# The last weight's first head in two passes of 128 tokens, in a one-core kernel of two transformer blocks

## What is computed

```python
def peer(x, w_q, sub_keys, expert_u, expert_v):
    q = (x @ w_q).reshape(B, S, 8, 2, 128)                      # 8 heads, two sides
    s = jnp.einsum('bshpk,hpnk->bshpn', q, sub_keys)            # 128 scores a side
    top_s, top_i = lax.top_k(s, 16)
    cand_s = top_s[..., 0, :, None] + top_s[..., 1, None, :]    # 256 pairs
    best_s, pos = lax.top_k(cand_s.reshape(B, S, 8, 256), 16)
    ids = (top_i[..., 0, :, None] * 128 + top_i[..., 1, None, :]) at pos
    g = jax.nn.softmax(best_s)
    # for each token, over its 8 * 16 = 128 experts:
    act = jax.nn.gelu(jnp.einsum('td,tkd->tk', x, expert_u[ids])) * g
    return jnp.einsum('tk,tkd->td', act, expert_v[ids])
```

## Time and profile before

| | |
|---|---|
| median of three runs | 3479.82 us (3477.35 to 3481.0) |
| the profiled execution, its own time | 3478.45 us |
| its span in the profile | 3476.6 us |
| TensorE clock granted, mean | 0.992 of 2.4 GHz |
| last split weight's matmuls end | about 2115.5 us |
| peer_w_q on TensorE | 2115.5 to about 2252.5 us |
| first gather issued | 2144.89 us |

### The profile page before, as it was taken

How to read it: one execution, slowest core, us unless ns; L and a number is a source line. 1 busy time by engine, 2 the same in 40 slices (tenths; PEclk the granted TensorE clock), 3 DMA queues, 4 the chain that set the end, 5 groups by cost and what they waited for, 6 DMA issues and landing times.

```text
span 3476.6 us, 34930 instructions
## 1 busy us (share of the span) xinstructions
PE 3131.9 (90%) x13518; PEld 2280.5 (66%) x13518; DVE 2235.2 (64%) x3468; ACT 1251.9 (36%) x1845; POOL 540.9 (16%) x533
## 2 busy tenths in 40 slices
PE   7999999999999999999999999898777767777776
PEld 6998998888877888888888888743222223222222
DVE  7786777775556777775557675757767554444444
ACT  5554566554435455554346752111111110000001
POOL 0000000000000000000000001535343333333332
PEclk9999999999999999999999999999999999999999
DMA  6554555556554655556565557999999999999998
GB/s 214 160 157 154 158 176 170 175 163 205 188 181 151 194 188 180 190 191 206 189 201 189 169 194 267 393 404 406 420 420 420 420 420 421 420 420 420 420 420 344
DMA packets 405740, 936.92 MB, mean 269 GB/s; under 512 B 16487, under 2 KB 246536, under 8 KB 339144
## 3 DMA queue, kind: packets, MB, share of 16 engines
q0 software_dynamic: 75936, 547.39, 38.3%
q1 hardware_dynamic: 328624, 386.96, 34.7%
q10 hardware_dynamic: 1016, 0.35, 0.0%
HBM read 932.54 MB, written 2.10 MB: 269 GB/s over the span
## 4 chain that ended last, share of the span: by engine, by line
PE 62%; DMA 28%; DVE 6%; POOL 2%; issue 1%; ACT 1%; POOLq 0%; ACTq 0%; SPq 0%; DVEq 0%
DMA Ub<-in_peer_u,ids 28%; PE W L1269 14%; PE W L1277 11%; PE W L1279 11%; PE W L1278 11%; PE W L1267 7%; DVE Ub L2324 4%; PE M L1330 1%; PE M L1419 1%; PE T L1419 1%; POOL Ub L2408 1%; PE W L1266 1%; DMA Vb<-in_peer_v,ids 1%; POOL Vb L2418 1%; PE W L1238 0%
## 5 line engine op out<-in xcount | busy, mean ns | idle before, releaser
L1901 DVE TENSOR_TENSOR wl<-raw,wh 128x1024 fp32r<-128x1024 f32 (+1 forms) x720 | 843.8, 1187 | 560.2 <-ACT wh L1502 558.3
L1502 ACT ACTIVATE wh<-raw 128x1024 fp32r<-128x1024 f32 (+1 forms) x720 | 730.2, 1029 | 754.3 <-PE W L1279 568.5
L2324 DVE CUSTOM_DVE_ANT_0 Ub<-Ub,xn 128x2048 f32<-128x2048 f32 x256 | 586.2, 2291 | 481.8 <-DMA Ub<-in_peer_u,ids 481.6
L1269 PE MATMUL W<-u,wh 128*128 128x512 f32 x2040 | 725.0, 398 | 0.0
L1419 PE MATMUL W<-Vb,diag 128*128 128x512 f32 x1008 | 465.3, 605 | 164.3 <-DMA Vb<-in_peer_v,ids 108.6
L1267 PE MATMUL W<-u,wl 128*128 128x256 f32 x2176 | 604.6, 283 | 4.6 <-DVE u L1863 4.6
L1277 PE MATMUL W<-wh,u 128*128 128x512 f32 (+1 forms) x1280 | 485.9, 380 | 1.2 <-DVE u L2252 1.0
L1279 PE MATMUL W<-wh,u 128*128 128x512 f32 (+1 forms) x1280 | 477.7, 373 | 0.0
L1278 PE MATMUL W<-wl,u 128*128 128x512 f32 (+1 forms) x1280 | 477.3, 373 | 0.0
L1419 PEld LDWEIGHTS W<-Vb,diag 128*128 128x128 f32 x1008 | 182.8, 191 | 446.7 <-issue 365.3
L1269 PEld LDWEIGHTS W<-u,wh 128*128 128x128 f32 x2040 | 384.8, 189 | 88.9
(11 more groups left out here) (332 smaller groups left out, 3022.2 us busy)
## 6 DMA issues: line engine op xcount, KB each, us to landing
raw<-in_w_in SPq DMA_DIRECT2D x128, 1024.0 KB, 5.3
raw<-in_w_up SPq DMA_DIRECT2D x88, 1024.0 KB, 5.4
raw<-in_w_down SPq DMA_DIRECT2D x44, 1024.0 KB, 5.0
raw<-in_w_in SPq DMA_DIRECT2D x144, 256.0 KB, 3.6
raw<-in_w_out SPq DMA_DIRECT2D x32, 1024.0 KB, 5.1
raw<-in_w_proj_a SPq DMA_DIRECT2D x16, 1024.0 KB, 5.0
Wb<-in_peer_w_q SPq DMA_DIRECT2D x16, 1024.0 KB, 9.4
raw<-in_w_proj_b SPq DMA_DIRECT2D x4, 1024.0 KB, 5.1
```

The costliest lines, as they stand in the source:

```text
L1269: i = q.matmul(o, vh, u[:, :, kk, :], start=False, stop=last)
L1502: q.activation(wh[:, s % NS, 0:b.half], r, ACT.Copy).then_inc(s_hi, 1)
L1901: q.tensor_tensor(wl[:, s % NS, 0:b.half], r, wh[:, s % NS, 0:b.half].bitcast(F32), SUB).then_inc(s_lo, 1)
L2324: q.tensor_tensor_reduce(U[:, :], U[:, :], xn[:, t, :], 1.0, 0.0, MUL, ADD, dots[t][:, k:k + 1]).then_inc(s_dot, 1)
```

## The change

Head 0 is taken out of the loop over the heads. `first_head` runs its 32 weight tiles twice, once with the first 128 tokens moving and once with the other 128. After the first pass ScalarE copies (`first_out`), TensorE makes the scores (`first_scores`, two matmuls), ScalarE keeps them (`first_keep`), and the first choice starts. `xn` is made in two halves, four pieces ahead and four (`second_xn`) when both passes are laid. `top_ids` treats both sides in one instruction each. Two more slots for chunks of peer_w_q lie over xn's second half and the second half of the scores; so chunks 0 and 1 go there, chunks 2 to 4 to the raw slots, 5 to 8 to the other four, and chunk i from 9 on waits for chunk i-7 as before.

```diff
-NW = 7
+NW = 9
+NWR = 7
@@ Plan
-        for i in range(8):
+        for j in range(4):
             yield "DVE", lambda: t
-            self.done("xn", self.put("DVE", 0.7, t, "xn", i % 2, i // 2))
-            if i < 7:
-                del self.ready["xn"]
+            self.done(("xn", 0, j), self.put("DVE", 0.7, t, "xn", 0, j))
+
+    def second_xn(self):
+        for j in range(4):
+            t = yield "DVE", lambda: self.when("first head")
+            self.done(("xn", 1, j), self.put("DVE", 0.7, t, "xn", 1, j))
@@ out_wq
-        if h == 0:
-            self.start((1, 0), self.choose(0, 0))
...
+    def first_head(self):
+        n = self.next_block
+        b = self.blocks[n]
+        self.until(lambda: self.pair_free[n % 2])
+        for t in range(2):
+            if t:
+                self.until(lambda: self.free(0.0, self.T0, self.T1))
+                self.first = self.T0.take(1), self.T1.take(1)
+            for k0 in range(0, 16, 2):
+                self.until(lambda: self.when(("turned", "u5", k0 // 2)))
+                self.pump()
+                s = b.first + k0 // 4
+                ready = max(self.loaded(s), self.when(("turned", "u5", k0 // 2)), self.pair_free[n % 2] if t == 0 else 0.0)
+                self.taken[s] = self.put("PE", 4 * 0.224, ready, "first", t, k0)
+            if t == 0:
+                self.pair_free[n % 2] = None
+            self.start((0, n), self.out_first(n, t, self.clock["PE"]))
+        self.done("first head", self.clock["PE"])
+        self.next_block += 1
+
+    def out_first(self, n, t, end):
+        yield "ACT", lambda: end
+        x = self.put("ACT", 0.5, end, "first_out", t)
...
+        x = yield "PE", lambda: None if self.when("keys") is None else self.free(x, bank)
...
+        x = self.done(("score", 0), self.put("PE", 0.45, x, "first_scores", t))
+        yield "ACT", lambda: None if self.when("peer") is None else x
+        bank.free = self.done(("sc0", t), self.put("ACT", 0.45, x, "first_keep", t))
+        if t == 0:
+            del self.ready["score", 0]
+            self.start((1, 0), self.choose(0, 0))
@@ choose
-        self.done(("ids", t, h), self.put("DVE", 3.6, r, "top_ids", t, h))
+        self.done(("ids", t, h), self.put("DVE", 3.1, r, "top_ids", t, h))
@@ lay
         self.start((2, 0), self.begin(128 - NU))
-        for h in range(8):
+        self.first_head()
+        self.start((1, 5), self.second_xn())
+        for h in range(1, 8):
             self.stream(("wq", h))
@@ sync
-                    if i < NR:
-                        e.wait_ge(s_lo, 2 * (c - NR) + 2)
+                    if i == 0:
+                        e.wait_ge(s_kym, 4)
+                    elif i == 1:
+                        e.wait_ge(*pair_done(("res", 2, 0)))
+                    elif i < 2 + NR:
+                        e.wait_ge(s_lo, 2 * (c - 2 - NR) + 2)
                     elif i < NW:
                         e.wait_ge(s_taken, plan.split_subs)
                     else:
-                        e.wait_ge(s_taken, 2 * (c - NW) + 2)
+                        e.wait_ge(s_taken, 2 * (c - NWR) + 2)
@@ tensor: first(t, k0)
+                for kk in (k0, k0 + 1):
+                    operand_ready(b, kk)
+                    for h in range(2):
+                        m = q.matmul((T0, T1)[h][:, 0:P] if t else pairs[n % 2][h][:, 0:P], w[:, kk % 8, col(h)],
+                                     u5[:, kk, col(t)], start=kk == 0, stop=kk == 15)
@@ vector: xn_part
+                if t:
+                    e.wait_ge(s_taken, taken_by(("wq", 0)))
@@ top_ids
-                for side in range(2):
...
+                q.tensor_scalar(pi[:, 0, :], pos[:, :], 4, None, ALU.logical_shift_right)
+                q.tensor_scalar(pi[:, 1, :], pos[:, :], 15, None, ALU.bitwise_and).then_inc(s_dve, me.up())
+                e.wait_ge(s_dve, me.n)
+                q.tensor_copy(pf[:, :, :], pi[:, :, :]).then_inc(s_dve, me.up())
...
+                q.tensor_tensor(oneh[:, :, :, :], strided(pf[:, :, :], [16, 2], [1, 16], [0, 16]),
+                                strided(iota[:, :], [0, 2], [0, 16], [1, 16]), ALU.is_equal).then_inc(s_dve, me.up())
...
+                q.tensor_tensor(oneh[:, :, :, :], oneh[:, :, :, :], strided(tif[:, :, :], [16, 2], [0, 16], [1, 16]), MUL).then_inc(s_dve, me.up())
...
+                q.tensor_reduce(sel[:, :, :], oneh[:, :, :, :], AX, ADD).then_inc(s_dve, me.up())
@@ dot, get_v
-                e.wait_ge(s_xn, 8)
+                e.wait_ge(s_xn, 4 * t + 4)
...
-                e.wait_ge(s_xn, 8)
+                if n:
+                    e.wait_ge(s_xn, 8)
```

More of the change, by code:

```diff
@@ L706, in out_wq @@
         self.sc[h] = (bank.name, bank.take(1))
+        self.in_order("scores of heads", h + 1)
         t = self.done(("score", h), self.put("PE", 0.9, t, "key_scores", h))
@@ L999, in program @@
         pos = area.get("pos", [16], U32)
-        pi = area.get("pi", [16], U32)
-        pf = area.get("pf", [16])
-        sel = [area.get(f"sel{i}", [16]) for i in range(2)]
+        pi = area.get("pi", [2, 16], U32)
+        pf = area.get("pf", [2, 16])
+        sel = area.get("sel", [2, 16])
         sg8 = area.get("sg8", [1])
@@ L1013, in program @@
         area = Area(raw0, Z)
-        Wb = [area.get(f"Wb{i}", [2048]) for i in range(NW)]
+        Wb = [at("Wsc", [2048], Z + 16384), at("Wxn", [2048], Z + 8192)] + [area.get(f"Wb{i}", [2048]) for i in range(2, NW)]
         area = Area(raw0, Z)
@@ L1081, in program, with slot, chunk_at @@
         CK = [slice(512 * j, 512 * (j + 1)) for j in range(4)]
-        slot_of = [(plan.split_subs // 2 + i) % NR for i in range(NR)] + list(range(NR, NW))
+        def slot(i):
+            return i if i < NW else i - NWR
+        def chunk_at(i):
+            i = slot(i)
+            return Wb[2 + (plan.split_subs // 2 + i - 2) % NR] if 2 <= i < 2 + NR else Wb[i]
         def col(k):
@@ L1240, in whole, with first, first_scores @@
                     m.then_inc(s_taken, 1)
+            def first(t, k0):
+                b = blocks[plan.at["wq", 0]]
+                n = plan.at["wq", 0]
+                i = k0 // 8
+                w = chunk_at(i)[:, :].rearrange("p (k n) -> p k n", n=b.n)
+                e.wait_ge(s_whole[slot(i)], 16)
+                if k0 == 0 and t == 0:
+                    e.wait_ge(s_pair[n % 2], plan.pair[n])
+                elif k0 == 0:
+                    e.wait_ge(s_T0, plan.first[0])
+                    e.wait_ge(s_T1, plan.first[1])
+                for kk in (k0, k0 + 1):
[3 more added lines that the diff above has]
+                                     u5[:, kk, col(t)], start=kk == 0, stop=kk == 15)
+                if t and k0 % 4 == 2:
+                    m.then_inc(s_taken, 1)
+                elif k0 == 14:
+                    m.then_inc(s_first, 1)
+            def first_scores(t):
+                name, before = plan.sc[0, t]
+                if t:
+                    e.wait_ge(s_T0, plan.first[0] + 1)
+                    e.wait_ge(s_T1, plan.first[1] + 1)
+                else:
+                    e.wait_ge(*pair_done(("wq", 0)))
+                e.wait_ge(s_M0, plan.key[8][1] + 1)
+                e.wait_ge(s_M1, plan.key[12][1] + 1)
+                e.wait_ge(s_bank[name], before)
+                for j in range(2):
+                    i = q.matmul(banks[name][:, col(j)], qTt[:, j, col(t)], kyT[:, j, :], start=True, stop=True)
+                i.then_inc(s_smm, 1)
             def sub(s, part):
@@ L1571, in out @@
                     if h >= 2:
[L1572 removed]
+                        e.wait_ge(s_smm, h)
                     for i in range(2):
@@ L2311, in top_weights @@
+                e.wait_ge(s_dve, me.n)
+                q.scalar_tensor_tensor(sel[:, 0, :], sel[:, 0, :], 128.0, sel[:, 1, :], MUL, ADD).then_inc(s_dve, me.up())
+                e.wait_ge(s_dve, me.n)
+                q.tensor_copy(ids[t][:, 16 * h:16 * h + 16], sel[:, 0, :]).then_inc(s_ids, 1)
             def top_weights(t, h):
```

76 lines of the change are left out of this document (46 added, 30 removed).

## The result

The kernel after takes **3489.04 us** (median of 7 runs, 3487.21 to 3494.18), the kernel before 3479.82 beside it (7 runs, 3477.35 to 3481.00): a ratio of 1.003, interval 1.0019 to 1.0042. It is slower by 9.2 us. The forecast was 3488 in 3476 to 3493. The profiled execution took 3488.22 us with a span of 3486.4.

The account below looks back on a forecast made before the run. The end was taken to follow peer_w_q's last block, delayed by ScalarE's order of gelus and copies. Profiled 3478.45 + 9.2 (later block) - 0.5 (ids) = 3487.2; median 1.4 over that execution: 3488, range 3476 to 3493.

Parts of the forecast that it names:

- The end follows ("wq", 7): Kernel's end follows the last block of peer_w_q, at 2252.55 before, since the spreads can't begin until it is done.
- G0 q2 G1 q3 G2 G3 q4 G4 q5 G5 G6 q6 q7: Forecast ScalarE order: G0 (dots 0 to 3) to G6 (24 to 27) are gelus, q0 to q7 copies to qTt.
- The first gather, 5.7 us earlier: First gather at 2139.2 against 2144.89: choice starts 4.8 earlier, ids save 0.9; bounds 3.5 and 6.6.
- I take none, as the idle is a third shorter: Forecast no clock drop after TensorE's 2.6 us wait between first-head pass inputs, though 4.04 us idle had halved it.
- The bound of 1.8: Extra us for the last 16 records of pass one if TensorE's clock halves; kept only for the range.
- Chunk 9 costs 3.0 us, so the groups come 2.7 earlier: Seven chunks instead of six share DMA with the gathers; one costs 3.0, leaving gelus 2.7 us earlier, bounds 0.5 and 6.6.
- q7 at 2261.8: Last peer_w_q block ends 15.9 after a copy held 5 us by its gelu: 9.2 us later than 2252.55.
- The 0.5 us from the ids near 2355: Of the other 15 top_ids calls only one may be on the path; saves 0 to 0.9, taken as 0.5.
- The old order: Rival: the last gelu, or two gelus, stay behind the copies as before; 3476.5, at best 3472.5; chance 0.17.
- DMA all along: Rival: DMA engines were the bound and start 5.7 us earlier; 3477 and less; chance 0.06.
- Only G3 moves: Rival: in ScalarE's list only the gelu of group 3 passes a copy; block 2.8 later, 3482; chance 0.12.
- The change without its gain: Rival: slices, half clock or second xn hold up pass one; gathers at most 2 us earlier; 3492; chance 0.10.

Follow-up runs that it names:

- Experiment 1: Kernel after with ScalarE's copies of heads 4, 5, 6 put back ahead of the gelus of groups 3, 4, 6 as before: 3483.69 us, ratio 1.0011.
- experiment 2: Kernel after with the copies of heads 3 to 7 moved ahead of the gelus they waited for in ScalarE's list: 3491.31 us, ratio 1.0035.
- experiment 3: Kernel before with only the new ScalarE order, gelus of groups 3, 4, 6 ahead of the copies of heads 4, 5, 6: 3486.92 us, ratio 1.0027.
- 4: Kernel before with the copies of heads 2 to 7 moved ahead of the gelus they waited for: 3488.33 us, ratio 1.0024.
- 5: Kernel after with VectorE's transposes (turns) of the first tokens' inputs laid ahead of the second normalisation xn: 3485.93 us, ratio 1.002.
- 6 (free, two queues): Kernel after with copies of heads 3 to 7 ahead of the gelus and chunks 10, 12, 14 issued from ScalarE's queue: 3477.26 us, ratio 0.9992.
- 7 (own list, two queues): Kernel after with its own ScalarE list and chunks 10, 12, 14 of peer_w_q issued from ScalarE's queue: 3489.09 us, ratio 1.0028.
- experiment 8: Kernel after with chunks 7 and 8 issued only once TensorE has taken chunks 0 and 1, undoing the preload in time: 3489.34 us.
- 9: Kernel after with turns ahead of second xn, copies of heads 3 to 7 ahead of gelus, and two chunk queues together: 3472.70 us, ratio 0.9979.
- 10: Kernel before with copies of heads 3 to 7 ahead of gelus and chunks 10, 12, 14 on ScalarE's queue: 3483.67 us, ratio 1.0009.
- 11: Kernel before with only the change's ids, both sides at once in each instruction: 3477.87 us, ratio 0.9995.
- 12: Kernel after, copies of heads 3 to 7 ahead of gelus, chunks 9 to 15 read as whole rows in wide packets (wrong weights, heads 4 to 7): 3479.35 us.

## Why the prediction was right, and where only in sum

*The end follows ("wq", 7).* Confirmed. From POOL's fourth gather of expert_v to the end of the span it is 3476.6 - 2252.78 = 1223.8 us before and 3486.4 - 2261.75 = 1224.7 after; in the experiments 1 to 12:

| experiment | fourth gather of expert_v | span | difference |
|---|---|---|---|
| 1 | 2268.11 | 3491.3 | 1223.2 |
| 2 | 2261.77 | 3489.7 | 1227.9 |
| 3 | 2259.98 | 3485.0 | 1225.0 |
| 4 | 2259.84 | 3487.2 | 1227.4 |
| 5 | 2257.15 | 3480.6 | 1223.5 |
| 6 (free, two queues) | 2250.60 | 3475.3 | 1224.7 |
| 7 (own list, two queues) | 2265.50 | 3488.7 | 1223.2 |
| 8 | 2262.48 | 3485.6 | 1223.1 |
| 9 | 2246.70 | 3474.4 | 1227.7 |
| 10 | 2253.93 | 3483.7 | 1229.8 |
| 11 | 2252.93 | 3476.0 | 1223.1 |
| 12 | 2253.50 | 3476.6 | 1223.1 |

Eight of the twelve lie within 2 us (1223.1 to 1225.0), while that gather moves by 17.5. The four others (2, 4, 9, 10) lie 2 to 7 us higher. In them the first spreads wait 2.0 to 9.4 us for `diag` (4, 9, 10), or POOL pauses 4.3 us (2). Waits of this kind also stand in 6 (2.61 and 2.26) and 12 (3.50), which are among the eight, so what makes the difference stays open.

*The list.* "G0 q2 G1 q3 G2 G3 q4 G4 q5 G5 G6 q6 q7" is the order of the trace, item for item, and experiment 3 shows it to be enough for 7.8 of the 9.2 us. One item was left out of the times: the exponential of head 1 stands between G3 and q4, and q4 came 1.73 us behind G3 (2208.37 against 2206.64), where the forecast has both at 2210.0. It cost nothing at the end, as q6 had to wait for G6 all the same.

*The first gather, 5.7 us earlier.* It was 4.17. The ids gave the 0.9 as worked out; the passes gave 3.26 in place of 4.8. The step that failed is "I take none, as the idle is a third shorter": after 2.44 us of idle TensorE ran at a mean granted clock of 0.66, between its two levels of 1.2 and 2.4 GHz, and 32 matmuls took 1.8 us more. The bound of 1.8 that was kept for the range is the value. In one launch of seven with the same idle the clock did not fall (experiment 8), and there the forecast of the start holds: the choice starts at 2128.77 (forecast 2129.0), and the first gather goes out at 2138.91 (forecast 2139.2). The Trainium skill (TensorE: Matmul & The Clock Gate, Part 1) says that idleness brings the throttle back. The traces agree in six of the seven.

*Chunk 9 costs 3.0 us, so the groups come 2.7 earlier.* They came 3.9 to 6.0 earlier (G3 2206.64 against 2212.66, G6 2244.44 against 2248.56). This step failed in kind. It charged the gathers with the chunks' bytes, as if both had to be done by a time; but bytes are given out by turns of packets, and the chunks are the ones that pay: landing takes a median of 46.1 us after the first gather (six chunks from 2146 to 2246), and TensorE waits for two of them.

*q7 at 2261.8.* It was 2261.51, and this closeness is luck in part. G6 came 1.5 us earlier than forecast and its stall was 3.35 in place of 5; from q6 to q7 it took 16.96 us in place of 15.9, as a chunk was 1.29 late.

*The 0.5 us from the ids near 2355.* Not shown. The profiled execution took 3488.22, 1.0 above the sum. q7 is 8.96 us later than before, and the end of the 54 groups of spreads 10.28: the first two groups ran at a granted clock of 0.50 to 0.65 here (3.28 us for the first, 1.96 before), which costs 1.7; the kernel before loses 0.4 at its fifth group, so 1.3 are left. The forecast had no term for it. Of the 10.28 some 0.5 is won back behind 2360; whether by the ids no run tells.

*The sum and its signs.* 3487.15 and 1.37 make 3488.5; the forecast says 3488. Of the signs, the first copy of ("wq", 7), the 33rd gather (2323.43) and the stalls came near their places, and the spreads end at 2359 and not at 2347. The DMA share was to be under 0.3 ahead of 2262: it is 0.46 in the 5 us from 2250 on and 0.00 in the next 5.

*The rivals.* "The old order" and "DMA all along" named 3476.5 and 3477. Experiment 1 sets the old order and finds 3483.7; experiment 2 takes away every wait of the list and finds 3491. Both rivals left out the waits for chunks that the gathers starve. Figures like theirs are reached only with a second queue (3477.3) or wide packets (3479.4). "Only G3 moves" did not happen. "The change without its gain" had its place in part: the half clock that it names is there.

Open: why the clock falls after the same idle in six launches and not in a seventh; and no run has the kernel after with the planner's costs themselves changed, so whether the planner would find the order of experiment 2 by other weights wasn't tried; nor was a chunk of twice the columns with right values.

## What to carry to other kernels

When one engine's list is laid out ahead, ask first what an earlier event does to the order, and then what stands right behind the wait that the order makes: here the list gave 3489 us and the starved chunks 3491, and free copies or a second queue alone measured as nothing. A latency-bound stream of small packets beside a bulk stream of large ones needs a share in packets, not bytes: count the packets of each queue in a window, and widen them or add a queue. An idle of 2.4 us ahead of a short critical stage on TensorE cost its own length here and, in six launches of seven, another 1.6 to 1.8 us in clock. And look where the profiled launch lies among the others before its waits are taken for those of the median.

## What the runs showed of the hardware

- The DMA engines serve queues one packet each while all have work: 991 against 991 packets with two queues, 861, 860 and 861 with three. The bytes go as the packets' sizes, 7.20 against 1.00 MB. The Trainium skill (DMA: Bandwidth & Descriptors, Queues, rings and completion order) says that an engine goes round its queues by packets. By that rule equal counts are what two full queues must show, and the trace agrees. The same page (Rules for kernel authors) says that spreading DMAs over issuing engines doesn't help bandwidth. The total stays indeed (410 GB/s with two queues, 401 with three), but the share of a starved stream went from 1.00 to 1.74 MB in 20 us, and with it 14 us of the time.
- In the kernel after a chunk of 1 MB landed 5.4 us after its issue at best, with no gather beside it, and 65.4 us at worst, beside gathers.
- After 2.44 us without work TensorE's granted clock had a mean of 0.66 over the next 5 us, and came back to 1.00 with no further pause; without that idle it was 1.00 throughout (experiments 5 and 9). With it the clock fell in six traces of seven; in that of experiment 8 it stayed at 1.00.
